# A gated conv and pooling layer on eight cores: the order of all engines from a list scheduler, the last stage of half 1 woven into half 2, transposes by DMA

## The reference, cut to what matters

```python
h = _rmsnorm(x, g_pre)
xa, ba, ca, za, xb, zb, ga, gb = jnp.split(h @ w_in, cuts, axis=-1)   # 8 x 1024 columns
# branch A: short gated causal convolution, width 3
u = ca * xa
conv = conv_b + sum(conv_w[k] * up[:, k:k + L] for k in range(3))     # up: history, then u
ya = ((ba * conv) * jax.nn.silu(za)) @ w_a_out
# branch B: trailing means over 2, 4, 8, 16 tokens by channel group, minus the token
d = (pooled - xb)                                                     # pooled: trailing mean of xb
mixed = jnp.einsum('blgc,gcd->blgd', d, w_grp) * pool_scale
yb = (mixed * jax.nn.silu(zb)) @ w_b_out
# merge, last stage
m = jax.nn.sigmoid(ga) * ya + jax.nn.sigmoid(gb) * yb
o = m @ w_o
x1 = x + _rmsnorm(o, g_post)
out = x1 + (p @ w_ple) * jax.nn.sigmoid(x1 @ w_pgate)
```

## Time and profile before

| | |
|---|---|
| runs shown | 848.89, 852.57, 869.7 us; median 852.57 |
| profiled execution: span of the slowest core (7) | 866.5 us; its own time is not given apart from the runs |
| spans of all cores | 842.3 to 866.5 us; core 0: 847.8 us |
| TensorE busy, core 7 | 800.5 us (92%) |
| VectorE, ScalarE, GpSimd busy | 341.2, 259.0, 333.0 us (39, 30, 38%) |

### The profile page before, as it was taken

The page is one execution under the profiler, slowest core; times in us unless marked ns, Lnnn a source line. Parts: engine busy times, 40 slices in busy tenths (PEclk is TensorE's granted clock), DMA queues, the critical chain, the costliest instruction groups (busy, mean ns, idle before and its releaser), DMA issues.

```text
span 866.5 us, 13521 instructions; the slowest of 8 cores (842.3 to 866.5 us)
## 1 busy us (share of the span) xinstructions
PE 800.5 (92%) x4238; PEld 385.9 (45%) x4238; DVE 341.2 (39%) x529; ACT 259.0 (30%) x468; POOL 333.0 (38%) x485
## 2 busy tenths in 40 slices
PE   1799999999999995998999999999989999979985
PEld 1344444444444443443444455545444545434442
DVE  2454444444121214666334445444542122224543
ACT  3532323232111124445222232322321311123432
POOL 3333344455423343444221243545543224214542
PEclk9999999999999997887788899999999999999998
DMA  9697565755664567444113432244224532313331
GB/s 212 146 129 108 79 107 83 102 84 79 105 97 64 89 113 176 149 140 146 50 16 58 73 61 44 45 73 74 50 50 65 107 65 50 55 52 104 104 107 70
DMA packets 37045, 77.60 MB, mean 90 GB/s; under 512 B 4052, under 2 KB 7252, under 8 KB 36978
## 3 DMA queue, kind: packets, MB, share of 16 engines
q0 software_dynamic: 29120, 48.31, 36.4%
q1 hardware_dynamic: 7858, 28.44, 9.8%
HBM read 115.77 MB, written 9.26 MB: 144 GB/s over the span
## 4 chain that ended last, share of the span: by engine, by line
PE 87%; DMA 4%; DVE 3%; issue 2%; ACT 1%; POOL 1%; SPq 0%; POOLq 0%; DVEq 0%; ACTq 0%
PE ps L526 40%; PE ps L674 26%; PE ps L830 8%; PE ps L757 6%; DMA arena<-xp 3%; PE ps L842 2%; DMA pb<-pp 2%; PE ps L635 2%; PE ps L504 1%; DVE x1T L817 1%; PE ps L809 1%; POOL arena L595 1%; PE ps L450 0%; ACT arena L885 0%; DVE qT L647 0%
## 5 line engine op out<-in xcount | busy, mean ns | idle before, releaser
L526 PE MATMUL ps<-hT,slab 128*128 128x512 bf16 (+1 forms) x1872 | 359.1, 356 | 0.0
L526 PEld LDWEIGHTS ps<-hT,slab 128*128 128x128 bf16 x1872 | 171.2, 100 | 185.3 <-issue 42.3
L674 PE MATMUL ps<-hT,slab 128*128 128x512 bf16 (+1 forms) x640 | 124.3, 347 | 2.4 <-ACT arena L885 1.4
L595 POOL TENSOR_TENSOR arena<-XB 128x526 f32<-128x526 f32 (+1 forms) x40 | 39.3, 982 | 211.6 <-ACT XB L574 189.2
L701 POOL TENSOR_TENSOR mT<-arena 128x512 bf16<-128x512 f32 (+1 forms) x40 | 44.1, 1103 | 157.5 <-DVE arena L697 156.5
L830 PE MATMUL ps<-wpg_sb,x1T 128*128 128x512 bf16 x272 | 75.4, 427 | 11.7 <-DVE x1T L817 11.7
L674 PEld LDWEIGHTS ps<-hT,slab 128*128 128x128 bf16 x640 | 57.5, 98 | 63.2 <-issue 3.1
L693 DVE TENSOR_TENSOR arena<-ps,arena 128x512 f32<-128x512 f32 (+1 forms) x40 | 24.4, 610 | 145.8 <-PE ps L674 145.1
L861 POOL TENSOR_TENSOR arena<-arena 128x512 f32<-128x512 f32 x34 | 55.9, 1644 | 61.5 <-DVE arena L856 56.5
L603 DVE SCALAR_TENSOR_TENSOR qT<-arena,XB 128x512 bf16<-128x512 f32 (+1 forms) x40 | 24.4, 611 | 117.1 <-POOL tail_x L616 55.6
L329 POOL DMA_DIRECT2D slab<-w_in x128 | 69.1, 557 | 2.0 <-issue 1.0
(11 more groups left out here) (86 smaller groups left out, 702.8 us busy)
## 6 DMA issues: line engine op xcount, KB each, us to landing
slab<-w_in POOLq DMA_DIRECT2D x128, 256.0 KB, 8.6
arena<-xp SPq DMA_DIRECT2D x32, 512.0 KB, 5.3
yp<-arena SPq DMA_DIRECT2D x16, 512.0 KB, 3.2
slab<-w_a_out POOLq DMA_DIRECT2D x16, 256.0 KB, 7.7
slab<-w_b_out POOLq DMA_DIRECT2D x16, 256.0 KB, 8.3
wo_sb<-w_o POOLq DMA_DIRECT2D x8, 256.0 KB, 5.3
wpg_sb<-w_pgate POOLq DMA_DIRECT2D x8, 256.0 KB, 5.3
pb<-pp POOLq DMA_DIRECT2D x16, 64.0 KB, 3.9
```

Source lines behind the costliest of these rows:

```text
L526: ins = e.matmul(bank(bi)[:, 0:N], lhsT=sl[:, sec, kk, :], rhs=hT[:, kk, k.rel:k.rel + N], start=(kk == 0), stop=(kk == 7))
L595: d(e.tensor_tensor(out=twin(out_i, k, nlo, E), in0=a, in1=b_, op=ALU.add))
L674: ins = e.matmul(bank(bi)[:, 0:N], lhsT=sl[:, sec, kk, :], rhs=act[:, kk, k.rel:k.rel + N], start=(kk == 0), stop=(kk == 7))
```

## The change

The whole program is rebuilt as a graph of operations. Each operation names its engine, what it reads and writes, an assumed duration (`dur`), for a DMA an assumed size (`mb`), and a `key`, a nominal time. `Graph.schedule` then lists the operations of each engine: again and again it takes, over all engines, the ready operation that could start first by the assumed times, and among those of one engine that could start equally early the one with the smallest key. Operations other than DMAs wait until their key is within 30 of the smallest key that is still open. Buffers come from pools (12 slab places, 4 of x, 9 temporaries, 8 PSUM banks, 3 bf16 rows, 2 of `x1T`, 2 of transposed p) and are given out during the listing. The order is fixed before the launch; at run time each engine executes its list and waits on semaphores. What else changes:

- `hT` is two buffers, one for each half; `wpg_sb` (`w_pgate`) takes the place of half 1's when that half's outputs are done, in four loads.
- Half 1's norms transpose on TensorE as before; half 2's norms, keyed into half 1's outputs, transpose by DMA from SP.
- The last stage takes x1 transposed by DMA from SP. Half 1's eight tiles are keyed from the start of half 2's projections on, 19 apart; the keys of these projections are stretched by 1.33. Half 2's tiles follow at 7.8.
- p comes transposed from the host; the small parameters come in one load, transposed on the host; the states are stored as they lie and rearranged on the host.
- Sigmoid becomes 0.5 (1 + tanh(x/2)): ACT computes tanh, DVE adds 1 and multiplies; the factor 0.5 goes into `w_ple` and, for the merge, out through the norm.
- The mean and the epsilon of the norms are folded into Square's scale and a small DVE operation.

Its core ("..." marks what is left out):

```diff
+    def schedule(self):
...
+            for e in ENGS:
+                te = t_eng[e]
+                cands = []
+                for o in avail[e]:
+                    if o.key > horizon and o.sem is None:
+                        continue
+                    st = max(te, o.ready)
...
+                lo = min(c[0] for c in cands)
+                st, o = min((c for c in cands if c[0] <= lo + 1e-6), key=lambda c: (c[1].key, c[1].i))
+                if best is None or st < best[0]:
+                    best = (st, o)
...
+            if o.sem is not None:
+                begin = max(st + o.dur + 1.2, dma_free)
+                dma_free = begin + o.mb / 0.29
+                o.done = dma_free + 0.8
+            else:
+                o.done = st + o.dur + (0.25 if o.eng == 'pe' else 0.12)
...
-        hT = sb("hT", [128, 8, NT], BF16)
+        hT = [sb("hT0", [128, 8, MAXP], BF16), sb("hT1", [128, 8, NT], BF16)]
...
+        wpg_sb = hT[0]
...
+        def phase0(tl, key, by_pe):
...
+            if by_pe:
...
+            else:
+                OP('sp', lambda e, d: d(e.dma_start_transpose(out=dst, in_=h.ap[:])), reads=[h], writes=[ht], sem=dsem(h, "tr"), dur=1.3, mb=0.3, key=key)
...
+        def phase3(tl, key):
...
+                OP('act', lambda e, d, b=b, h=h: d(e.activation(out=xb.ap[:, h * 512:(h + 1) * 512], in_=b.ap[:, :], func=AF.Square, scale=1.0 / 32.0, accum_out=stat(3 + h, gi))),
+                   reads=[b, res("stats")], writes=[xb, ss[h]], dur=0.8, key=key + 1.7 * (h + 1))
...
+            OP('act', lambda e, d: d(e.copy(out=xb.ap[:], in_=x.ap[:])), reads=[x], writes=[xb], dur=1.05, key=key + 7)
+            xT = val(p_xT)
+            OP('sp', lambda e, d: d(e.dma_start_transpose(out=xT.ap[:], in_=xb.ap[:])), reads=[xb], writes=[xT], sem=dsem(xT, "tr"), dur=1.3, mb=0.3, key=key + 8)
...
+                OP('pe', f_g, reads=[xT] + [res(f"wpg{kk}") for kk in range(8)], writes=[bg], dur=1.726, key=key + 12 + 2.2 * h)
...
+                OP('act', lambda e, d, t=t, bg=bg: d(e.activation(out=t.ap[:, 0:512], in_=bg.ap[:, :], func=AF.Tanh, scale=0.5)),
+                   reads=[bg], writes=[t], dur=0.6, key=key + 14 + 2.2 * h)
+                OP('dve', lambda e, d, t=t, be=be: d(e.scalar_tensor_tensor(out=t.ap[:, 0:512], in0=t.ap[:, 0:512], scalar=1.0, in1=be.ap[:, :], op0=ALU.add, op1=ALU.mult)),
+                   reads=[be], writes=[t], dur=0.69, key=key + 14.5 + 2.2 * h)
...
+        for n, tl in enumerate(i1.tiles):
+            phase0(tl, t2 + 2 + 10.0 * n, False)
+        t = run_phase2(i0, t2, LEAD, STEP)
...
+        for k0 in range(0, 8, 2):
+            load_res("wpg", wpg_sb, w_pgate, k0, k0 + 2, t3 + 1.5 * k0, extra=old_h)
+        P3SP = 19.0
+        for n, tl in enumerate(i0.tiles):
+            phase3(tl, t3 + 14 + P3SP * n)
+        t = run_phase1(i1, t3, LEAD, STEP, stretch=1.33)
...
+        t = run_phase2(i1, t5, LEAD, STEP)
+        for n, tl in enumerate(i1.tiles):
+            phase3(tl, t + 7.8 * n)
+
+        G.schedule()
```

More of the change, by code:

```diff
@@ new lines, with __init__, pick @@
+class Buf:
+    __slots__ = ('name', 'ap', 'tenant', 'free_at', 'guard')
+    def __init__(self, name, ap, guard=()):
+        self.name = name
+        self.ap = ap
+        self.tenant = []
+        self.free_at = 0.0
+        self.guard = list(guard)
+class Pool:
+    def __init__(self, name, bufs):
+        self.name = name
+        self.free = list(bufs)
+    def pick(self):
+        best = None
+        for b in self.free:
+            if any(v.left for v in b.guard):
+                continue
+            at = max([b.free_at] + [o.done for v in b.guard for o in v.ops])
+            if best is None or at < best[0]:
+                best = (at, b)
+        return best
@@ new lines, with op @@
+class Op:
+    __slots__ = ('i', 'eng', 'emit', 'dur', 'lat', 'key', 'preds', 'nsucc', 'vals', 'first', 'sem', 'n_dma', 'mb',
+                 'start', 'done', 'npred', 'succs', 'ready', 'seq', 'clk')
+class Graph:
+    WINDOW = 30.0
+    def __init__(self):
+        self.ops = []
+    def op(self, eng, emit, reads=(), writes=(), dur=0.1, key=0.0, sem=None, n_dma=1, mb=0.0, after=()):
+        o = Op()
+        o.i = len(self.ops)
+        o.eng, o.emit, o.dur, o.key, o.sem, o.n_dma, o.mb = eng, emit, dur, key, sem, n_dma, mb
+        o.preds = set(after)
@@ L63, in op @@
         for r in reads:
-            add(r.lw, True)
-            if r.pending > 0:
-                r.pending -= 1
+            o.preds.update(r.lw)
         for w in writes:
[L68 to L78, removed]
@@ L79, in op @@
-        seq = self.cnt[clk]
+            o.preds.update(w.lw)
+            o.preds.update(w.rd)
+        o.vals = list(dict.fromkeys(list(reads) + list(writes)))
         for w in writes:
-            w.lw = (clk, seq)
-            w.rs = {}
+            w.lw, w.rd = [o], []
         for r in reads:
[L84 to L90, removed]
@@ new lines, in emit @@
+    def emit(self, nc, stack):
+        cnt = {}
+        for e in ENGS:
+            for o in self.order[e]:
+                if o.sem is None:
+                    o.clk, inc = e, 1
+                else:
+                    o.clk, inc = o.sem(), 16 * o.n_dma
+                o.seq = inc
+        for o in sorted(self.ops, key=lambda o: (o.start, o.i)) if False else [o for e in ENGS for o in self.order[e] if o.sem is None]:
+            cnt[o.clk] = cnt.get(o.clk, 0) + o.seq
+            o.seq = cnt[o.clk]
+        for o in sorted((o for o in self.ops if o.sem is not None), key=lambda o: (o.start, o.i)):
+            cnt[o.clk] = cnt.get(o.clk, 0) + o.seq
+            o.seq = cnt[o.clk]
+        sems = {c: stack.enter_context(nc.semaphore("s_" + c)) for c in cnt}
@@ L188, in res @@
             if name not in R:
-                R[name] = Res(name)
+                R[name] = Val(name)
             return R[name]
[L192 to L200, removed]
@@ L222, in build_program @@
[L222 to L237, removed]
@@ L253, in f_invcnt @@
             d(ins)
[L254 to L271, removed]
@@ L530, in phase1_unit @@
-            b_xa, b_ca, b_ba, b_za, b_xb, b_zb = banks
+            rr = hres(sbi, k)
+            act = hT[sbi]
+            b_xa, b_ca, b_ba, b_za, b_xb, b_zb = [group(ws[s], act, rr, k, key + dk * i) for i, s in enumerate((S_XA, S_CA, S_BA, S_ZA, S_XB, S_ZB))]
             cw = lambda t: smallT[:, j, t:t + 1]
             cbias = smallT[:, j, 3:4]
-            psc = smallT[:, j, 4:5]
             sm = res("smallT")
-            ur = ures("U", k)
-            xr = ures("XB", k)
-            prev_u = [ures("U", info.blocks[k.idx - 1])] if (not k.samp and k.idx > 0) else []
@@ new lines, in phase1 @@
+            OP('act', lambda e, d: d(e.activation(out=blkview(t_sz.ap, k), in_=blkview(b_za.ap, k), func=AF.Silu)), reads=[b_za], writes=[t_sz], dur=a_ps, key=key + 4 * dk)
+            OP('dve', lambda e, d: d(e.tensor_tensor(out=actview(vT, j, k), in0=blkview(t_c.ap, k), in1=blkview(t_sz.ap, k), op=ALU.mult)),
+               reads=[t_c, t_sz], writes=[res(f"vT{j}_{k.idx}")], dur=d_t, key=key + 4 * dk)
+            OP('act', lambda e, d: d(e.copy(out=uwin(XB, k, 16, E), in_=blkview(b_xb.ap, k))), reads=[b_xb], writes=[xr], dur=a_ps, key=key + 5 * dk)
```

1033 lines of the change are left out of this document (412 added, 621 removed).

## The result

The changed kernel takes 808.46 us (median of four, 808.28 to 814.25), the kernel before 850.23 beside it; the ratio of the means is 0.952, 95% interval 0.948 to 0.957. The prediction was 807, with 784 to 850. The profiled execution took 808.56; its slowest core, core 3, spans 807.0.

The account below looks back on a forecast made before the run. TensorE was taken to bound the kernel: 735.4 us of matmuls plus losses of 28 (head), 4 (half 1), 14 (weave), 4 (half 2) and 17 (end) make 802.4; with 4.8 offset, 807. Range 784 to 850.

Parts of the forecast that it names:

- Dense weave: Half 1's last stage among half 2's projections: the 39.5 loss goes, late transposed tiles bring back 14 us.
- the lateness of 1.7: Each of eight woven tiles: landing 5.5 against the modelled 4.3, 1.2 later, plus 0.5 for drift.
- The rival of late transposes: TensorE waits before each woven gate matmul; a landing of 10 gives 853, from 11.8 slower by 2%; chance 0.13.
- The head: Kernel start: first projection at 24.2 instead of 26.67, loss 28 instead of 31.3, ends 24 and 31.
- I leave the rest: Head: twelve early weight slabs instead of six and four x buffers instead of six were given no cost.
- The half clock of the first group: Head: the first projection group runs at half clock, 3.57 us instead of 1.73, and this stays.
- the 39.5: Loss in us in half 1's last stage before the change; all predicted to go, with projections to run in between.
- The end: Last stage of half 2: loss 17 us instead of 31.2, ends 12 and 33.
- the rest of half 2: Half 2's projections and outputs: loss falls from 9.3 to 4.0 us.
- no TensorE work for the state outputs: Half 2: four transposing state outputs go, two plain stores instead, saving 5.3 us of TensorE.
- The offset: 4.8 us added at the end: median of runs, 852.57, above core 0's span of 847.8.
- The clock rival: Denser matmuls bring core 7's granted clock of 0.81 to every core, giving 980 us; chance 0.03.

Follow-up runs that it names:

- e7_early: Changed kernel, with the scheduler believing each transposed x1 tile of a last stage lands 2 us earlier than in its plan: 822.54 us, 14.1 more.
- e1_plan: Changed kernel, with the scheduler told that x loads of tiles 4 to 7 land 12 us after issue; loads issued as before: 796.12 us, 12.3 less.
- e9_both: Changed kernel with the edits of e1_plan and e2_pool together: 795.55 us, 0.6 under e1_plan.
- e2_pool: Changed kernel, with loads on POOL's queue made to obey the 30 us horizon, so early weight loads are held back: 804.72 us, 3.7 less.

## Why the prediction was right, and which steps were not

*Dense weave, right; its size, wrong.* The term was 8 x (1.2 + 0.5) = 14; the weave lost 6.2. The landing itself was not shorter than the 5.5 that I took: the eight tiles of the weave landed after 4.6, 3.9, 13.6, 5.6, 7.9, 3.1, 3.1 and 7.2 us (mean 6.1, median 5.1). The step that failed is the lateness of 1.7 on each of the eight tiles: it set 5.5 against a modelled 4.3 for all of them. The model puts transposes behind weight loads in its one queue; worked out from the kernel, its landings for these tiles are 4.3, 4.3, 9.7, 4.6, 7.3, 4.3, 4.3 and 5.0, mean 5.5, and it leaves 0.1 to 1.7 between a landing and its gate matmul. So four tiles of eight were waited for, 4.0 together, and 1.7 more went where the clock fell behind the longest wait:

```profile
408.82 5.30 PE L657 MATMUL ps<-hT,x1T 128*128 128x512 bf16 x16 [1.98 <-DMA x1T<-hb]
```

What lands later than listed does stop TensorE, as predicted (e7_early). The rival of late transposes was half true, one landing of 13.6, and cost little, because the listing had 9.7 for it. The Trainium skill, "VectorE: DVE Perf Modes", section on the three transpose paths, would have made a landing about 12.5 with the hand-over, an estimate from eight blocks; this trace has 3.1 on its quickest tiles, so its figure for one block doesn't add up block after block here.

*The head, wrong.* Predicted: first projection at 24.2, 28 in all, fewer x buffers and more slabs left out of account. Measured: 27.95, and 44.6 with half 1. The step that failed is "I leave the rest": the extra loads do something to the plan as well as to the DMA. About 10 of the 12.6 is the planned landing of four tiles (the ledger of e1_plan has 10.4 less by 310 us), 2 to 4 the traffic (e9_both, e2_pool). The copy did come first, as predicted, but the fourth tile's transposes stood at 25.89 instead of 22.31, because its x landed later. The half clock of the first group was read from its 3.57 us alone: the records of the granted clock begin only at 32.6 in that trace, so the 1.00 of the row says nothing of it. Eight matmuls of the same length stood at 0.53 in the changed kernel, from 51.62 on.

*What took the 39.5 away, wrong in its cause.* The prediction put it down to the projections that run in between. The weave is worth 8 to 10; the moved norms 9; the scheduler's order, with the small parts that no run takes from it, 18. The sum didn't notice, because it went by the whole.

*The end, right in the sum only:* 19.0 for 17, the wait on the last tile 4.5 for 5. But the low clock cost 2.9 for 1.6, TensorE's last matmul was 10.6 from the end for 6.8, and the waits of 3.5 were 0.7. *Right:* the rest of half 2, no TensorE work for the state outputs, the loads of the gate weights hidden (no wait of TensorE on them), no table loads. *The offset,* 4.8, was 1.5: an execution's time lies 1.5 to 1.6 beyond the span of its own slowest core, and the other 3.3 came of taking core 0 of one execution against the median of others.

*The clock rival* did not occur: the cores of the changed kernel had mean clocks of 0.982 to 0.988 with TensorE dense from 62 to 718. Behind the last wait of 4.46 the final 16 gate matmuls took 6.47 instead of 3.61, at a granted clock of 0.55, near the lower level (1.2 GHz).

## What to carry to other kernels

A list scheduler's order is only as good as the landing times it believes: compare planned with measured landings before changing what is loaded. Hold loads to the same horizon as the work that they feed (3.7 by itself here, 0.6 beside the right plan), and behind the small operations that share their issuing engine. Compare landings stage by stage: a median over all tiles hides the one that is waited for. When one change has many parts, undo them one by one; the part that it is named after may carry a fifth of what a stage gained.

## What the runs showed of the hardware

A DMA transpose of a 128 x 1024 bf16 tile landed 3.1 to 13.6 us after its issue, with a median of 5.1 in the weave (DMA share 0.57) and 3.8 in the last stage (0.47). In the first 60 us the DMA ran at a share near 1.00 and about 195 GB/s, and 0.5 MB loads of `w_o` queued there on POOL's queue took 45 us to land, while loads of x of the same size on SP's queue beside them took 4.4 to 18.4, 9.7 in the median. Behind waits of 1.98, 4.46 and 5.13 us TensorE's granted clock was 0.68, 0.55 and 0.57 over the sixteen matmuls that followed, and these took 5.30, 6.47 and 6.26 us instead of 3.61. Twenty table loads of 1283 ns in an engine busy under a third cost no time.
